# Loading X as two token tiles in 64-row halves, with four warm-up products, at the head of a two-layer transformer kernel

## The reference, cut to what matters

```python
def token_mixer(x, w_in, b_forget, rel_bias, w_out):
    proj = x @ w_in                       # x: (1, 256, 1024)
    q_a, k_a, v_a, f_a, q_b, k_b, v_b = jnp.split(proj, SPLITS, axis=-1)
    log_f = jax.nn.log_sigmoid(f_a + b_forget)
    y_a = forgetting_attention(q_a, k_a, v_a, log_f)
    y_b = chunked_band_attention(q_b, k_b, v_b, rel_bias)
    return concat_heads(y_a, y_b) @ w_out

def reference(...):
    x = layer_norm(ALPHA1 * x + token_mixer(x, ...))
    x = layer_norm(ALPHA1 * x + conv_ffn(x, ...))
    x = layer_norm(ALPHA2 * x + retention_mla_layer(x, ...))
    return layer_norm(ALPHA2 * x + moba_layer(x, ...))
```

## Time and profile before

| What | us |
| --- | --- |
| median of 3 runs | 745.34 |
| lowest and highest of them | 744.3 and 745.77 |
| the profiled execution, by the same clock | 745.1 |
| its span (first to last instruction) in the trace | 743.3 |
| busy time of PE in it | 732.5 |

### The profile page before, as it was taken

One profiled execution on the slowest core, in us unless ns is written; L12 is line 12 of the kernel. 1 busy time (PEld: TensorE's weight loads), 2 busy tenths in 40 slices (PEclk: granted clock), 3 DMA queues, 4 the chain that ended last, 5 costly groups with the idle time before them and its releaser, 6 DMA issues.

```text
span 743.3 us, 11949 instructions
## 1 busy us (share of the span) xinstructions
PE 732.5 (99%) x4444; PEld 638.9 (86%) x4444; DVE 546.8 (74%) x952; ACT 395.0 (53%) x644; POOL 44.5 (6%) x57
## 2 busy tenths in 40 slices
PE   8999999999999999999999999999999999999995
PEld 7898977888888888789899888988888879999884
DVE  4766677799999855868686557966574588879665
ACT  5576671787777654165544554343443424555650
POOL 0000001021111200100000000000000010000002
PEclk9999999999999999999999999999999999999999
DMA  8864372467555596265445443553585616544612
GB/s 287 288 244 142 119 251 85 170 202 249 185 193 171 166 330 217 95 212 177 138 150 175 142 142 114 174 191 127 188 271 194 222 49 229 169 129 157 199 36 78
DMA packets 37193, 131.13 MB, mean 176 GB/s; under 512 B 4296, under 2 KB 4688, under 8 KB 37008
## 3 DMA queue, kind: packets, MB, share of 16 engines
q1 hardware_dynamic: 35136, 124.30, 49.9%
q0 software_dynamic: 1552, 5.51, 2.6%
q10 hardware_dynamic: 448, 0.56, 0.2%
HBM read 129.30 MB, written 1.06 MB: 175 GB/s over the span
## 4 chain that ended last, share of the span: by engine, by line
PE 97%; DVE 1%; DMA 0%; DVEq 0%; issue 0%; SPq 0%
PE acc L960 25%; PE acc L962 24%; PE acc L961 24%; PE acc L1011 10%; PE acc L1012 5%; PE acc L1119 2%; PE acc L1139 2%; PE acc L1109 2%; PE acc L1076 1%; PE acc L1158 1%; PE acc L1171 1%; DMA res<-in_x 0%; PE acc L1132 0%; PE acc L1182 0%; DVE small L1708 0%; DVE res L1732 0%
## 5 line engine op out<-in xcount | busy, mean ns | idle before, releaser
L1488 DVE TENSOR_TENSOR w_lo<-raw,w_hi 128x1024 fp32r<-128x1024 f32 (+2 forms) x219 | 261.0, 1211 | 68.7 <-ACT w_hi L1284 65.8
L1284 ACT ACTIVATE w_hi<-raw 128x1024 fp32r<-128x1024 f32 (+2 forms) x219 | 224.4, 1044 | 75.0 <-PE acc L962 61.3
L960 PE MATMUL acc<-X,w_hi 128*128 128x256 f32 (+1 forms) x528 | 152.4, 289 | 0.0
L962 PE MATMUL acc<-X,w_lo 128*128 128x256 f32 (+1 forms) x528 | 149.6, 283 | 0.0
L961 PE MATMUL acc<-X,w_hi 128*128 128x256 f32 (+1 forms) x528 | 149.5, 283 | 0.0
L1011 PE MATMUL acc<-X,w_hi 128*128 128x512 f32 x320 | 111.2, 392 | 0.0
L960 PEld LDWEIGHTS acc<-X,w_hi 128*128 128x128 f32 (+1 forms) x528 | 100.4, 190 | 2.5 <-issue 1.7
L960 PE MATMUL acc<-w_hi,S_hi 128*128 128x512 f32 x256 | 101.3, 396 | 0.0
L961 PEld LDWEIGHTS acc<-X,w_hi 128*128 128x128 f32 (+1 forms) x528 | 100.4, 190 | 0.6
L962 PEld LDWEIGHTS acc<-X,w_lo 128*128 128x128 f32 (+1 forms) x528 | 100.3, 190 | 0.3
L961 PE MATMUL acc<-w_lo,S_hi 128*128 128x512 f32 x256 | 99.8, 390 | 0.0
(11 more groups left out here) (203 smaller groups left out, 964.2 us busy)
## 6 DMA issues: line engine op xcount, KB each, us to landing
raw<-in_w SPq DMA_DIRECT2D x228, 512.0 KB, 4.2
gate<-in_ln_gain POOLq DMA_DIRECT2D x4, 512.0 KB, 4.3
gate<-in_ln_bias POOLq DMA_DIRECT2D x4, 512.0 KB, 5.1
gate<-in_bias SPq DMA_DIRECT2D x1, 1024.0 KB, 8.4
out<-res SPq DMA_DIRECT2D x4, 256.0 KB, 2.1
res<-in_x SPq DMA_DIRECT2D x3, 256.0 KB, 5.0
raw<-in_w SPq DMA_DIRECT2D x3, 256.0 KB, 3.7
rot<-cum POOLq DMA_DIRECT2D x1, 512.0 KB, 4.2
```

The costliest lines, as they stand in the source:

```text
L960: nc.tensor.matmul(out, a_hi, b_hi, start=start, stop=False)
L962: return nc.tensor.matmul(out, a_lo, b_hi, start=False, stop=stop)
L1284: nc.scalar.activation(home(u, "hi")[:, 0:n], raw[:, u % RAW, 0:n], ACT.Copy).then_inc(hi_done, 1)
L1488: nc.vector.tensor_tensor(home(u, "lo")[:, 0:n], raw[:, u % RAW, 0:n], home(u, "hi")[:, 0:n].bitcast(F32), ALU.subtract).then_inc(lo_done, 1)
```

## The change

X now comes as token tiles: both halves of the features in one row of 4 KB, and each token tile in two DMAs of 64 rows. SP issues rows 0 to 63 of both tiles, ACT issues rows 64 to 127. There is one semaphore for each token tile (`x_in[tt]`), and a transpose of either half of the features waits for the whole tile (32 counts, from two DMAs). The identity moves from SP's queue to the head of ACT's. Weight piece 1 comes in one DMA of 512 KB on SP, and the split of its first half waits for all of it. SP now waits for token tile 1 before pieces 2 to 4. The first group of warm-up products has four in place of three.

```diff
-        def load_x(eng, tt, q):
-            v = slice(q * 512, (q + 1) * 512)
-            eng.dma_start(res[:, tt, v], t["x"][0, tt * P:(tt + 1) * P, v]).then_inc(x_in[2 * tt + q], 16)
+        def load_x(eng, tt, half):
+            p0 = 64 * half
+            eng.dma_start(res[p0:p0 + 64, tt, :], t["x"][0, tt * P + p0:tt * P + p0 + 64, :]).then_inc(x_in[tt], 16)
...
                 if step == ("load", "start"):
-                    sp.dma_start(ident, t["const"][:, 0:P]).then_inc(ident_in, 16)
-                    for tt, q in ((0, 0), (0, 1), (1, 1)):
-                        load_x(sp, tt, q)
-                    sp.dma_start(raw[:, 1, 512:1024], t["w"][1, :, 512:1024]).then_inc(landed[1], 16)
-                    sp.wait_ge(x_in[2], 16)
+                    load_x(sp, 0, 0)
+                    load_x(sp, 1, 0)
+                    load_piece(1)
+                    sp.wait_ge(x_in[1], 32)
                     for u in range(2, RAW):
                         load_piece(u)
...
                     if tj["needs"] == 0:
-                        pe.wait_ge(x_in[2 * tt + q], 16)
+                        pe.wait_ge(x_in[tt], 32)
                         pe.wait_ge(ident_in, 16)
...
-                for _ in range((3, 1)[n]):
+                for _ in range((4, 1)[n]):
                     nc.tensor.matmul(acc[:, 3, 0:256], rtmp[:, 1, 256:256 + P], rtmp[:, 1, 256:512], start=True, stop=True)
...
+            act.dma_start(ident, t["const"][:, 0:P]).then_inc(ident_in, 16)
+            load_x(act, 0, 1)
             act.dma_start(raw[:, 0, 0:piece_size(0)], t["w"][0, :, 0:piece_size(0)]).then_inc(landed[0], 16)
-            load_x(act, 1, 0)
-            act.dma_start(raw[:, 1, 0:512], t["w"][1, :, 0:512]).then_inc(half_landed, 16)
+            load_x(act, 1, 1)
             act.dma_start(bforget, t["b_forget"]).then_inc(bf_in, 16)
             for step in ORDER:
                 if step == ("split_hi", 1, 0):
-                    act.wait_ge(half_landed, 16)
+                    act.wait_ge(landed[1], 16)
                     nc.scalar.activation(w_hi[:, 1, 0:512], raw[:, 1, 0:512], ACT.Copy).then_inc(half_hi, 1)
                 elif step == ("split_hi", 1):
-                    act.wait_ge(landed[1], 16)
                     nc.scalar.activation(w_hi[:, 1, 512:1024], raw[:, 1, 512:1024], ACT.Copy).then_inc(hi_done, 1)
```

More of the change, by code:

```diff
@@ L770, in build @@
         const_in, ident_in, bias_in = sem("const_in"), sem("ident_in"), sem("bias_in")
-        half_landed, half_hi, half_lo = sem("half_landed"), sem("half_hi"), sem("half_lo")
-        x_in = [sem(f"x_in{i}") for i in range(2 * NT)]
+        half_hi, half_lo = sem("half_hi"), sem("half_lo")
+        x_in = [sem(f"x_in{i}") for i in range(NT)]
         cum_done, cum_out = sem("cum_done"), sem("cum_out")
```

## The result

The changed kernel is slower: 750.29 us, the median of four runs (749.45 to 750.47), against 744.82 of the kernel before on the same chip (four runs, 743.89 to 745.77). The ratio is 1.0073, with a 95% interval from 1.0061 to 1.0085; +5.5 us in place of the -0.5 that was forecast.

A forecast was written before the change was run, and what follows sets the result against it. PE's work, or its start, was taken to bound the kernel. Second transposes 0.5 us later but a faster clock gave -0.54: 745.1 to 744.56 for the profiled execution, plus 0.24 for the median, 744.8 us; range 743.8 to 746.3.

The forecast's parts named there:

- Where to look: Whole kernel: PE is busy in 732.5 of 743.3 us, so the whole question lies in the first 13 us.
- The fourth warm-up product at nothing: PE before the first transposes: one more product fits into the 0.80 us of waiting for X and costs nothing.
- Token tile 0 at 4.7 to 5.0: First transposes: about as many bytes ahead (576 KB) as before, so they start at 4.7 to 5.0 us; counted 0.
- Token tile 1 at 6.2: Second transposes: wait for all of X's second tile, start at 6.2 us, 0.5 later than before, bounds 0 and 1.4.
- the late bound of 7.1: X's second tile at the earlier trace's rates: 1.25 MB passed at 6.5 us, landing at 7.1.
- The clock: TensorE at the head: risen when the second transposes start, not at about 9.5 us; twelve products take 1.41, not 1.95.
- Weights at nothing: Pieces 1 to 4 and ACT's splits: later landings hidden, piece 0's split has until 6 us; counted 0.
- The sum: End of piece 0's twelve products at 9.71 us in place of 10.25: -0.54 on everything after it.
- the prediction's own chain: From the second transposes: four at 0.11 us, 1.66 to the first product, 1.41 for the twelve products.
- the slower rival: Head: X's second tile at 7.1 us, PE's break of 1.4 keeps the clock low; +2.0, 747.3 us; chance 0.11.
- The rule of the Trainium skill that the prediction weighed: X's transfers: partition halves share the same 16 engines and bring nothing; second tile at 7.1, +0.35, 745.7 us; chance 0.14.

## Why the prediction was wrong, step by step

**Where to look** held: the head of the program, X's transfers, PE's first break. The loss is there to a few tenths.

**The fourth warm-up product at nothing** held, in both kernels: the transposes still waited for X, 0.15 in the one and 0.77 in the other. Nothing measurable was gained by the fuller PE either.

**Token tile 0 at 4.7 to 5.0** missed by 0.7: the transposes start at 5.66. This was hidden behind tile 1.

**Token tile 1 at 6.2** is the term that failed: 9.9, and 2.8 beyond the late bound of 7.1. Three things were wrong in it.

First, the rates. The bounds were 420 GB/s and the rates of the earlier trace rows, and both belong to transfers over all 128 partitions. Halves of 64 rows moved 210 to 303. Summed over the windows, 1.25 MB, the bytes that I had counted up to X's last, had passed at 6.8, where the earlier trace rows gave 6.5; the bytes behind these met the wider gap, 303 and 258 GB/s against 393 and 428.

Second, the bytes. I counted what lies ahead of X's last half in its own queue and as much in the other. But ACT's queue fell behind SP's: its identity and piece 0 go in small rows, 512 and 256 bytes, and its first half of X landed 1.3 after SP's, though issued only 0.4 later. So SP was through with its halves when ACT still had one to send, and piece 1 came in beside it. X's last byte was the last of all 1.67 MB that had been issued, not of 1.25. The experiment without piece 1 on SP's queue took 1.7 off tile 1's landing and 2.6 off the time. Neither of the two outweighs the other by the runs: columns in place of halves, with all the bytes, took 1.9 off the landing and 2.2 off the time, whole tiles 2.7 and 3.2.

Third, a row was passed over. The earlier trace rows has the quarter that SP issued at 2.1 landing 5.5 later, at 7.6, and it completes tile 1. I noted that nobody waited for it, and then set 7.1 as the late end for a change by which PE does wait for it. The experiment with the waits alone shows what that row was worth: tile 1 complete at 7.5, tile 0 at 6.4, +2.1 us.

**The clock** rose as I took it, and sooner: the transposes at 5.66 were fast. The reason that I had given for it, the filled break, was not borne out, since with three warm-up products and a longer break it rose sooner still (4.6); that it came true was luck. And the step ended there. With tile 1 at 9.9 the break ahead of the second transposes was 3.62 and not 0.5, and the clock fell in it. Transposes and products went at the low level, worth some 1.8 at the head by the experiment that fills the break; the 1.0 in the time is within the noise. Against the kernel before it is less, +0.6 for the twelve products, because five and a half of its twelve were slow too.

**Weights at nothing** held in its own terms: after the second copy ACT went on to split piece 1 without a wait. It failed in what the weights do to others: piece 1 to X, as above, and piece 0, whose split at 6.88 came after the 6 that I had named. In the changed kernel that was hidden behind tile 1; in the kernel with waits by quarters it was the bound.

**The sum and the rivals.** With the measured landing the prediction's own chain gives 9.9 for the transposes, +4.2, and twelve products at 0.213 add 0.6: +4.8, of the +5.0 at the first product over 128 columns. So the slower rival had the right mechanism (a late tile, a break, the low clock through the products), and its size was off by its landing of 7.1. The rule of the Trainium skill that the prediction weighed ("DMA: Bandwidth & Descriptors", section "Rules for kernel authors": two transfers to disjoint halves of the partitions aren't worth it) speaks of no gain. Here it was a loss: +2.2, +2.8 and +3.2 us in the three pairs that differ by the halves (against columns, in the order of the queues before, and against whole tiles), by the ratios +2.0, +2.2 and +2.9. The landings of the earlier trace rows that the prediction set beside that rule were of quarters over all 128 partitions, and could say nothing of halves. The rule on ports, cited above, was the one to draw on.

**What costs how much.** The parts don't add up, since each acts through the latest arrival. Against the kernel before with four warm-up products (744.54), by medians, the waits for whole tiles alone cost 2.1, the new order of the queues 2.7 (with it the undivided piece 1 and SP's wait, which no run parts from it), both together 3.5, and both with 64-row halves, which is the change, 5.75.

## What to carry to other kernels

Before a wait is widened from a part to a whole, read in the trace when the whole lands today: that landing is the first estimate, whatever the new order promises. Cut a transfer along its columns and not along its partitions if it must be cut at all, and when two queues feed one consumer, ask which queue will lag and what the other sends meanwhile. A gain at the head of a program is kept only as far as the next path that was just in time before.

## What was not expected of the hardware

Half of a 512 KB piece, over 64 partitions and with the other half behind it, took 3.3 to 3.5 us to land, and the whole piece over 128 took 3.1 to 3.3.

A queue with small rows falls behind: 32 KB in rows of 256 bytes took 2.2 us at the head of a queue, and 4.9 to 5.8 in the middle of one, beside large rows on the other queue. The packets show the two queues taking turns by packets and not by bytes. From 2.5 to 4.0 us of the kernel with whole tiles SP's sent 109 packets and ACT's 113, but 0.41 and 0.06 MB; from 2.5 to 3.5 us of the one with columns each sent 140, 0.26 and 0.07 MB. In the changed kernel, with halves in both queues, the counts are not equal (88 and 148 from 4.5 to 6.0 us).

The clock first rose anywhere from 4.1 to 13.7 us in the profiled executions of these kernels, and at 9.5, 7.0 and 4.1 in three that are alike up to there but for one warm-up product. No run settled what decides it.
